# Moving the scaling of the one-hot rows earlier in ScalarE's program, in the expert scoring of a retrieval block

## The reference

```python
s1, i1 = lax.top_k(sc[:, :, 0], PEER_TOPK)
s2, i2 = lax.top_k(sc[:, :, 1], PEER_TOPK)
cand = (s1[..., :, None] + s2[..., None, :]).reshape(T, PEER_HEADS, PEER_TOPK * PEER_TOPK)
best, ci = lax.top_k(cand, PEER_TOPK)
idx = e1 * PEER_N_KEYS + e2
g = jax.nn.softmax(best.astype(jnp.float32), axis=-1)
u_sel = jnp.take(u_tab, idx, axis=0)
act = jax.nn.gelu(jnp.einsum('td,thkd->thk', xb, u_sel))
v_sel = jnp.take(v_tab, idx, axis=0)
return jnp.einsum('thk,thkd->td', g.astype(act.dtype) * act, v_sel)
```

## Time and profile before

| | |
|---|---|
| median of 3 runs | 1693.98 us (1693.87 to 1694.13) |
| the profiled execution's own time | 1694.13 us |
| its span in the profile | 1692.3 us |
| PE busy | 1663.5 us, 98% |
| PEld, DVE, ACT, POOL busy | 1483.3, 1424.9, 959.6, 528.6 us |
| granted TensorE clock, mean | 0.995 |

### The profile page before, as it was taken

One profiled execution on the slowest core, in us unless ns is written; L12 is line 12 of the kernel. 1 busy time (PEld: TensorE's weight loads), 2 busy tenths in 40 slices (PEclk: granted clock), 3 DMA queues, 4 the chain that ended last, 5 costly groups with the idle time before them and its releaser, 6 DMA issues.

```text
span 1692.3 us, 25455 instructions
## 1 busy us (share of the span) xinstructions
PE 1663.5 (98%) x9286; PEld 1483.3 (88%) x9286; DVE 1424.9 (84%) x2056; ACT 959.6 (57%) x1517; POOL 528.6 (31%) x335
## 2 busy tenths in 40 slices
PE   9999999999999999999999999999999999999995
PEld 7887778878999999999999999988888888888884
DVE  4545777468799998999998999779999999999995
ACT  5554566453466567777775555555555555555554
POOL 0001310015330102232223444104565545455554
PEclk9999999999999999999999999999999999999998
DMA  7765544576566768787778999989999999999992
GB/s 234 218 186 174 148 149 158 193 254 207 189 230 230 270 229 274 269 269 266 276 261 309 400 396 400 317 317 402 400 381 410 404 399 397 396 402 397 400 394 94
DMA packets 135722, 494.87 MB, mean 292 GB/s; under 512 B 15424, under 2 KB 15456, under 8 KB 135088
## 3 DMA queue, kind: packets, MB, share of 16 engines
q1 hardware_dynamic: 95760, 347.65, 57.9%
q0 software_dynamic: 39552, 145.07, 22.6%
q10 hardware_dynamic: 288, 0.55, 0.1%
HBM read 487.86 MB, written 5.34 MB: 291 GB/s over the span
## 4 chain that ended last, share of the span: by engine, by line
PE 94%; DVE 2%; DMA 2%; ACT 1%; issue 1%; DVEq 0%; SPq 0%; ACTq 0%
PE PS L1683 20%; PE PS L1689 12%; PE PS L1725 7%; PE PS L1727 7%; PE PS L1726 7%; PE PS L1732 7%; PE PS L1733 7%; PE PS L1428 6%; PE PS L1435 6%; PE PS L1454 4%; PE PS L1431 3%; PE PS L1439 3%; PE PS L1667 3%; PE PS L1464 2%; DMA RING_RAW<-u_t 2%
## 5 line engine op out<-in xcount | busy, mean ns | idle before, releaser
L760 ACT ACTIVATE HI<-V_RAW 128x1024 fp32r<-128x1024 f32 x256 | 271.9, 1062 | 269.8 <-PE PS L1727 217.7
L1683 PE MATMUL PS<-xT,HI 128*128 128x384 f32 x2048 | 410.4, 341 | 1.5 <-ACT HI L760 1.1
L1683 PEld LDWEIGHTS PS<-xT,HI 128*128 128x128 f32 x2048 | 347.4, 189 | 3.8 <-ACT HI L760 2.8
L525 POOL DMA_INDIRECT PICKED<-peer_u,PK x128 | 202.1, 1579 | 472.2 <-DVE DOTS L1299 455.6
L1240 DVE TENSOR_TENSOR V_LO<-V_RAW,HI 128x2048 fp32r<-128x2048 f32 x128 | 295.8, 2311 | 55.2 <-ACT HI L760 55.1
L760 ACT ACTIVATE HI<-RING_RAW 128x1024 fp32r<-128x1024 f32 x256 | 270.5, 1057 | 125.3 <-DMA RING_RAW<-u_t 121.9
L1247 DVE TENSOR_TENSOR RING_LO<-RING_RAW,HI 128x1024 fp32r<-128x1024 f32 x249 | 294.7, 1220 | 7.3 <-ACT HI L760 7.1
L525 POOL DMA_INDIRECT PICKED<-peer_v,PK x128 | 209.8, 1639 | 193.8 <-DVE ACC L1304 166.6
L1689 PEld LDWEIGHTS PS<-xT,RING_LO 128*128 128x128 f32 x2048 | 263.8, 191 | 0.9 <-DVE RING_LO L1247 0.9
L1689 PE MATMUL PS<-xT,RING_LO 128*128 128x192 f32 x2048 | 263.9, 271 | 0.5 <-DVE RING_LO L1247 0.5
L912 DVE TENSOR_TENSOR LO<-RAW,HI 128x1024 fp32r<-128x1024 f32 x121 | 150.5, 1245 | 120.8 <-PE PS L1435 99.3
(11 more groups left out here) (219 smaller groups left out, 2062.9 us busy)
## 6 DMA issues: line engine op xcount, KB each, us to landing
RING_RAW<-u_t SPq DMA_DIRECT2D x256, 512.0 KB
V_RAW<-peer_v SPq DMA_DIRECT2D x256, 512.0 KB, 7.5
RAW<-w_in SPq DMA_DIRECT2D x80, 512.0 KB, 3.7
RAW<-w_out SPq DMA_DIRECT2D x32, 512.0 KB, 4.4
RAW<-wq_t SPq DMA_DIRECT2D x32, 512.0 KB, 4.6
x_spill<-X POOLq DMA_DIRECT2D x2, 1024.0 KB, 5.9
PICKED<-peer_u,PK POOLq DMA_INDIRECT x128
PICKED<-peer_v,PK POOLq DMA_INDIRECT x128
```

The costliest lines, as they stand in the source:

```text
L525: pool.indirect_dma_start(PICKED[slot][:], None, table.rearrange("e (a c) -> (e a) c", a=2), bass.IndirectOffsetOnAxis(PK4[:, half, g:g + ...
L760: nc.scalar.activation(HI[:, n % HI_SLOTS, :], raw_of(n), ACT.Copy).then_inc(top_ready, 1)
L1683: return mm(PS[:, j % S_BANKS, 0:2 * ND].rearrange("p (a t) -> p a t", a=2), HI[:, n % HI_SLOTS, kk * P:(kk + 1) * P], xT[:, k, :, 0:ND], ...
```

## The change

`gates_into(b)` moves from step b+38, where it stood between `top` and `put_gates`, to the end of step b+37, behind `put_gates`. The computation and all semaphores stay as they were; DVE, PE, POOL and SP keep their lists.

```diff
                 if j != NKEYS - 2:
                     top(2 * j + 6)
-                if 0 <= j + 1 - SPREAD0 < N_BATCH:
-                    gates_into(j + 1 - SPREAD0)
                 if 0 <= j - SPREAD0 < N_BATCH:
                     put_gates(j - SPREAD0)
                 if j in GATES_AT:
                     gates_exp(GATES_AT.index(j))
                 if j in PICKS_AT:
                     picks_to_rows(PICKS_AT.index(j))
+                if 0 <= j + 2 - SPREAD0 < N_BATCH:
+                    gates_into(j + 2 - SPREAD0)
```

## The result

The changed kernel is slower: 1704.12 us median (1702.75 to 1705.45) against 1694.06, ratio 1.0054 with a 95% interval of 1.0041 to 1.0067, so 9.2 us with an uncertainty of some 2. The medians are 10.1 us apart; 9.2 is the distance of the means of the six runs on either side. The forecast was 1703.0 with a range of 1697.5 to 1707. The profiled execution took 1703.53 us, 9.4 more than that of before.

The account below looks back on a forecast made before the run. PE, at 5.48 us a step, was taken to set the time; -0.5 + 0.1 + 9.6 = +9.2 us gave 1703.2 on the median, stated as 1703.0 us, with an 8-in-10 range of 1697.5 to 1707.

Parts of the forecast that it names:

- DVE's 14.9 us of waits: From 654 to 909 us, DVE's `land` waits 16 times for ACT's `put_gates`; removing this was claimed worth nothing.
- Gain of 0.50 at the second spread: PE's wait at the second `spread` goes, as `gates_into(1)` runs a step earlier: -0.50 us.
- ring: Once-a-step loop of DVE and ACT (`sum_halves`, `apply_gates`, `one_hots`, `gates_into`, `low_half_out`): 5.63 to 5.80 us against PE's 5.48.
- hop from DVE to ACT: From the end of `one_hots` on DVE to the start of `gates_into` on ACT: 0.04 us.
- copy to the sum: From the start of `low_half_out` on ACT to `sum_halves` on DVE: 0.43 us.
- slack: Time a unit is ready before PE wants it: 0.93 us at step 41, overdrawn by 0.05 at batch 7.
- excess: What the ring takes over PE's step: 0.146 + 0.004 b us; 9.6 us over batches 8 to 45.
- rival 3: ACT's `top` ahead of `put_gates` waits for late loads and lengthens the ring: 4 us more, 1707; chance 0.07.
- rivals 1 and 2: PE's slack holds: no cost, 1693.5 us, chance 0.11; or about half the cost, 1697 to 1700 us, chance 0.08.
- rival 1: `one_hots` ends before ACT comes to `gates_into`, so only the -0.50 is left: 1693.5 us; chance 0.11.

Follow-up runs that it names:

- e3: The changed kernel with one of the four scalings in each `gates_into` left out: ratio 0.9996 to the kernel before.
- e1: The changed kernel with `gates_into` placed one copy later, right behind `low_half_out` and still ahead of `top`: ratio 0.9997 to the kernel before.
- e2: The kernel before with `gates_into(b)` kept in step b+38 but moved behind `put_gates`: ratio 1.0002 to the kernel before.

## Why the prediction was right

- *PE sets the time in the stage, and DVE's 14.9 us of waits are worth nothing.* Held: they fell to 0.9 in a slower kernel and to 7.4 in one that is no faster.
- *Gain of 0.50 at the second spread.* Measured 0.53 in the four kernels that have the gain and no cost. The matmul's idle 0.26 us understated it: the weight load waited too (0.43 us) and was not hidden. The sum that the prediction worked out by the page "TensorE: Matmul & The Clock Gate" of the Trainium skill (a gain of 0.26) does not hold here.
- *A ring of 5.63 us at first and 5.80 at last.* Measured 5.60 at batch 1 and 5.79 near the end. The hop from DVE to ACT, taken from another pair of instructions as 0.04, is 0.03 (657.09 + 1.22 = 658.31 to 658.34). The copy to the sum is 0.40 against 0.43.
- *PE feels it from batch 7 on, which overdraws the slack by 0.05.* Held to the step: the first late unit is 99, prepared in step 47 behind the copy that ends batch 7's turn of the ring, and PE's step with it is 5.59, so 0.11 over. That the step is met exactly is in part luck. The slack was smaller than forecast, 0.76 against 0.93 (`top(87)` ends at 660.78 and its weight load starts at 661.59, less a hop of 0.05), and the excess that used it up was smaller too.
- *9.7 us of excess (0.1 and 9.6), 9.2 with the gain taken off.* Measured 9.10 (281.31 less the 272.21 of the kernels without a cost and without a late spread) and 8.57. The ring was overrated by 0.03 at first and 0.01 at last: from step 47 to 85 DVE's sums lie 217.23 us apart, an excess of 0.234 a step where 0.252 was forecast, 0.7 us in all, of which the earlier end of the slack gives a little back. The profiles differ by 9.4 us, and the 0.8 that the stage doesn't explain lies outside it (1.0 more behind it, 0.2 less ahead of it), within the scatter there. So the total of 9.2 came out nearer than its terms, by luck.
- *Late loads would lengthen the ring (rival 3).* They don't. Before, the list of waits from 654 to 909 us has the row below, and in the changed kernel's list of the stage there is none of this kind. ACT comes later and finds the loads landed.

```profile
ACT HI L760 <- DMA RING_RAW<-u_t: 22.6, 20, 2.4
```

- *The slack might hold (rivals 1 and 2).* It does for eight batches, and for some fourteen when the ring closes in the middle, and then it is used up. With one scaling fewer rival 1 would have been the truth, as e3 shows: the margin was 0.12 to 0.31 in 5.7 (5.60 and 5.79 against 5.48).

What a reader of the waits alone would have missed: PE's rows in the list of waits add up to 3.9 us (2.3 and 1.6), its matmuls' busy time misses only 0.5 of 265 and its weight load's 6.0, while its rhythm lost 9.1. The ends of matmuls are modelled in these records, so busy time can hide small gaps; the starts show the whole loss.

## What to carry to other kernels

Before an instruction is moved so that it waits for something made in the same step, follow the step's dependencies all the way round: if they come back to their own beginning by way of a queue's order, the sum of that ring is a lower bound of the step, and it must be compared with the step of the engine that sets the time. Below that it costs nothing, whatever waits the trace shows in it; above it each step costs the excess, once the slack of the buffers is used up, so a test on a few steps shows nothing. To shorten the ring, put between two members of it only what belongs to it: behind the copy the same scaling was free.

## What the runs showed of the hardware

POOL's issue of a gather (L525) in the stage took 1891 ns in the mean before and 979 ns after, though neither the instruction nor its count (41) changed. Spans on POOL are rough in these records, but the two lengths below repeat within some hundredths of a microsecond. The rows of the changed kernel around one of them:

```profile
704.86 0.94 POOL L525 DMA_INDIRECT PICKED<-peer_u,PK  x1 [4.71 <-DVE DOTS L1299]
704.95 0.36 DVE L1256 TENSOR_TENSOR TMP<-PS,HOLES 128x192 f32<-128x192 f32 x1 [0.37 <-issue]
705.23 2.35 DVE L1247 TENSOR_TENSOR RING_LO<-RING_RAW,HI 128x1024 fp32r<-128x1024 f32 x2
```

and of e1, where DVE goes on at once (its sum starts at 702.91, in the rows above):

```profile
703.27 1.94 POOL L525 DMA_INDIRECT PICKED<-peer_u,PK  x1 [3.54 <-DVE DOTS L1299]
```

The issue is short where POOL began before DVE's subtraction of two SBUF tiles (L1247), which it does where DVE stood idle ahead of its sum: in 39 of the 41 issues of the changed kernel it began 0.22 to 0.49 us before and took 0.94. It is long where that subtraction was already under way: in 38 of the 41 of the kernel before it began some 0.08 us behind the subtraction's start and took 1.94 to 1.95. The means go with it: 1918 ns in e1, 1819 in e2, and 1183 in e3, where POOL comes first, or within 0.03 us of the subtraction's start, in most steps. The page "SBUF — State Buffer" of the Trainium skill, section "SBUF: two separate sides", says that a DVE instruction with two SBUF inputs and a POOL instruction that reads SBUF lock each other out, and that the one that starts first blocks the other for its whole length. The rows fit that in one direction only. The subtraction that begins while POOL's issue is under way isn't held up: it starts 0.28 us behind the sum's start (704.95 to 705.23), against 0.27 in e1 (702.91 to 703.18), and one takes 1.22 us with an issue under way or without. No run here separates the lock from another cause, and the longer issue costs nothing here, since POOL waits for DVE anyway.
